# An expert loop over pairs, written out and pipelined, with a flipped token gather, a 14-slot weight ring and 8 KB rows

## The reference: an attention block with 16 experts, then a second block

```
cap = CAPACITY_FACTOR * seq // N_EXPERTS            # 2*512/16 = 64 tokens per expert
aff = softmax(h @ w_router)                          # 512 x 16
gate, idx = top_k(aff.T, cap)                        # per expert: 64 tokens and their gates
xe = h[idx]                                          # 16 x 64 x 1024
a  = silu(xe @ w_gate[e]) * (xe @ w_up[e])           # 1024 -> 1024, twice
ye = (a @ w_down[e]) * gate[..., None]
y  = zeros(512, 1024).at[idx].add(ye)                # scatter back, added to x
```

## Time and profile before

| | |
|---|---|
| median of three runs | 1732.81 us (1731.86 to 1734.91) |
| profiled execution, span from first to last instruction | 1732.2 us (no other time is recorded for this execution) |
| PE busy | 1569.3 us, 91% |
| VectorE, ScalarE, GpSimd busy | 574.1, 474.7, 100.6 us |
| DMA queue of SP | 304.14 MB, 47.0% of the 16 engines' span |
| the eight passes of the expert loop on PE | from 459.6 to 974.5 us |

### The profile page before, as it was taken

The page is one execution under the profiler, slowest core; times in us unless marked ns, Lnnn a source line. Parts: engine busy times, 40 slices in busy tenths (PEclk is TensorE's granted clock), DMA queues, the critical chain, the costliest instruction groups (busy, mean ns, idle before and its releaser), DMA issues.

```text
span 1732.2 us, 18849 instructions
## 1 busy us (share of the span) xinstructions
PE 1569.3 (91%) x7428; PEld 1006.7 (58%) x7428; DVE 574.1 (33%) x1061; ACT 474.7 (27%) x855; POOL 100.6 (6%) x118
## 2 busy tenths in 40 slices
PE   6959959988499999999999789998989899999998
PEld 3434526633234434434434479996767688888886
DVE  0145365442401211211211462112556433344334
ACT  2143236611211011011101331124763433213321
POOL 2000030000000000000000120000002211000100
PEclk9979969998799999999999899998989999999999
DMA  5279360012199999999999302214011132233221
GB/s 204 30 247 380 125 230 1 2 60 75 49 402 380 384 408 377 387 405 393 387 408 381 120 25 73 74 50 146 1 37 49 49 97 98 97 98 97 98 73 49
DMA packets 105457, 305.15 MB, mean 176 GB/s; under 512 B 7052, under 2 KB 43173, under 8 KB 103346
## 3 DMA queue, kind: packets, MB, share of 16 engines
q1 hardware_dynamic: 104712, 304.14, 47.0%
q0 software_dynamic: 512, 0.09, 0.1%
q10 hardware_dynamic: 170, 0.05, 0.0%
HBM read 300.07 MB, written 4.19 MB: 176 GB/s over the span
## 4 chain that ended last, share of the span: by engine, by line
PE 83%; DVE 6%; ACT 4%; POOL 2%; DMA 2%; issue 1%; SPq 1%; ACTq 0%; DVEq 0%; POOLq 0%
PE ps L683 19%; PE ps L725 11%; PE ps L726 11%; PE ps L727 11%; PE ps L448 4%; PE ps L671 4%; PE ps L613 3%; PE ps L713 3%; PE ps L809 2%; PE ps L566 2%; ACT sb L946 2%; PE ps L574 2%; DMA sb<-in_w_mod 2%; PE ps L489 1%; PE ps L589 1%
## 5 line engine op out<-in xcount | busy, mean ns | idle before, releaser
L683 PE MATMUL ps<-sb 128*64 128x512 f32 x1536 | 334.9, 594 | 13.3 <-ACT sb L946 13.3
L683 PEld LDWEIGHTS ps<-sb 128*64 128x64 f32 x1536 | 110.1, 137 | 221.7 <-issue 214.3
L946 ACT ACTIVATE sb<-ps 128x512 f32<-128x512 f32 (+5 forms) x217 | 104.3, 485 | 423.1 <-PE ps L683 163.9
L725 PE MATMUL ps<-r_act,r_top 128*128 128x512 f32 x352 | 138.3, 393 | 3.5 <-POOL r_act L1885 2.3
L727 PE MATMUL ps<-r_act,r_low 128*128 128x512 f32 x352 | 137.3, 390 | 0.0
L1759 DVE TENSOR_TENSOR r_low<-raw,r_top 128x2048 fp32r<-128x2048 f32 x33 | 74.4, 2293 | 79.9 <-ACT r_top L946 79.9
L1582 DVE TENSOR_TENSOR sb<-sb,ps 128x512 f32<-128x512 f32 x16 | 11.0, 688 | 253.5 <-PE ps L683 253.5
L726 PE MATMUL ps<-r_low,r_mid 128*128 128x512 f32 x240 | 93.4, 389 | 0.0
L725 PE MATMUL ps<-r_low,r_h 128*128 128x256 f32 x320 | 90.7, 283 | 0.0
L726 PE MATMUL ps<-r_low,r_h 128*128 128x256 f32 x320 | 90.6, 283 | 0.0
L727 PE MATMUL ps<-r_low,r_top 128*128 128x256 f32 x288 | 81.5, 283 | 0.0
(11 more groups left out here) (353 smaller groups left out, 2393.4 us busy)
## 6 DMA issues: line engine op xcount, KB each, us to landing
sb<-in_w_gate SPq DMA_DIRECT2D x64, 1024.0 KB, 17.9
sb<-in_w_up SPq DMA_DIRECT2D x64, 1024.0 KB, 11.2
sb<-in_w_down SPq DMA_DIRECT2D x64, 1024.0 KB, 12.6
sb<-in_w_mod SPq DMA_DIRECT2D x16, 1536.0 KB, 9.4
raw<-in_f_w_up SPq DMA_DIRECT2D x22, 1024.0 KB, 7.7
raw<-in_a_w_in SPq DMA_DIRECT2D x12, 1024.0 KB, 5.4
raw<-in_f_w_down SPq DMA_DIRECT2D x5, 2048.0 KB, 7.7
sb<-in_w_in SPq DMA_DIRECT2D x4, 1440.0 KB, 10.6
```

The lines of the kernel that those rows point to most:

```text
L683: mm = pe.matmul(PS[64 * hf:64 * hf + 64, b * HALF:(b + 1) * HALF], lhsT(k), ring[:, c % RINGN, kk, hf * HALF:(hf + 1) * HALF], start=(k = ...
L725: pe.matmul(o, a_hi, b_hi, start=first, stop=False)
L946: return act_(o, i_, ACT.Identity, bias=bias, scale=scale)
```

## The change

The loop over pairs becomes straight code with another order on PE, SP, ScalarE and VectorE.

- **Gather flipped.** `onehot` (fp32r) is now the loaded operand, and the token rows, split once into `h2hi` and `h2lo`, are the moving one, 512 columns at a time: 16 fp32r matmuls for a pair (`gather`, after-line L648). Four small ones (L653) fetch the gate of each slot into `gcol`. The result `xe` has tokens on partitions, and eight transposes (`turn_xe`, L664) turn it. ScalarE makes `h2hi` with four copies, VectorE `h2lo` with four subtractions, ahead of the loop.
- **Gate folded.** The expert output is multiplied by `gcol` and split into `yehi` (ScalarE) and `yelo` (VectorE). `GT` is a plain one-hot, and the scatter is 16 fp32r matmuls (L684, L685) over two PSUM banks instead of four. The matmul L665 is gone, L663 is now fp32r (L720).
- **Pipelined.** The gather of the next pair stands behind this pair's fourth matrix, its transposes ahead of the sixth. The scatter of the last pair is spread behind eight chunks of matrices 2 and 3.
- **Ring.** 14 slots instead of 12. Partition p now takes rows 2p and 2p+1 of a chunk, one row of 8 KB (`expert_load`, L2008); the transposes read every second column to match.
- **Ends.** Slot numbers run from 1, which drops L1548 and the copy L1534. `xc` is loaded behind the last chunk, into slot 10, and normalised by ScalarE and VectorE inside the last pair. The first three weight pieces of the second block are issued right behind it.

```diff
-RINGN = 12
+RINGN = 14
...
+            def gather(i):
+                pe.wait_ge(*at("x_onehot", i))
+                for hf in range(2):
...
+                        for part in (h2hi, h2lo):
+                            mm = pe.matmul(bank(6 + hf), onehot[:, t, :], part[t][:, hf * HALF:(hf + 1) * HALF],
+                                           start=(t == 0 and part is h2hi), stop=(t == NT - 1 and part is h2lo))
...
+            for i in range(PAIRS):
...
+                weights(i, 0, claim(0, ("x_sil", (i, 0))), tokens(0))
+                weights(i, 1, claim(1, ("x_act", (i, 0))), tokens(0), adds=0)
+                weights(i, 2, claim(2, ("x_sil", (i, 1))), tokens(1), adds=4)
+                turn_act(i, 0)
...
+                weights(i, 3, claim(0, ("x_act", (i, 1))), tokens(1))
+                if i + 1 < PAIRS:
+                    gather(i + 1)
+                pe.wait_ge(*at("x_aT", (i, 0)))
+                weights(i, 4, claim(1, ("x_ye_a", (i, 0)), ("x_ye_d", (i, 0))), hidden(0))
+                turn_act(i, 1)
+                if i + 1 < PAIRS:
+                    turn_xe(i + 1)
+                pe.wait_ge(*at("x_aT", (i, 1)))
+                weights(i, 5, claim(2, ("x_ye_a", (i, 1)), ("x_ye_d", (i, 1))), hidden(1))
+            for n in range(8):
+                scatter(PAIRS - 1, n)
```

On ScalarE, in each pair (the `else` branch is the last pair):

```diff
+                copy(actT[:, 0, :, :], bank(3).rearrange("p (k q) -> p k q", k=4)).then_inc(*inc("x_aT", (i, 0)))
+                if i + 1 < PAIRS:
+                    x_rows(i + 1)
+                else:
+                    eng.wait_ge(*at("xc_in"))
+                    for t in range(NCT):
+                        a = act_(sb(T16 + t * D, D), xc[t], ACT.Square, accum_out=ssq[:, 12 + t:13 + t])
+                    a.then_inc(*inc("ssqc"))
+                    eng.wait_ge(*at("rsce"))
+                    act_(rs[:, 12:14], rs[:, 12:14], ACT.Sqrt).then_inc(*inc("rscs"))
+                eng.wait_ge(*at("x_pe_aT", (i, 1)))
+                copy(actT[:, 1, :, :], bank(3).rearrange("p (k q) -> p k q", k=4)).then_inc(*inc("x_aT", (i, 1)))
```

On SP, the layout of a chunk and the end of the loads:

```diff
-            gate = [I[n].rearrange("a e (c j p) f -> (a e) c p j f", p=P, j=2) for n in ("w_gate", "w_up", "w_down")]
+            experts = [I[n].rearrange("a e (c p j) f -> (a e) c p (j f)", p=P, j=2) for n in ("w_gate", "w_up", "w_down")]
...
+            for c in range(12, NCHUNK):
+                expert_load(c)
+            sp.wait_ge(*at("x_used", NCHUNK - RINGN))
             for t in range(NCT):
                 sp.dma_start(xc[t], I["ctx_2"][0, t * P:(t + 1) * P, :]).then_inc(*inc("xc_in", 0, 16))
```

More of the change, by code:

```diff
@@ L116, in value @@
         return self.known.get((name, key), 1)
[L120 to L138, removed]
     def result(self):
-        return {**self.here, **{("total", n): c for n, c in self.count.items()}}
+        return dict(self.here)
 def constants():
     ident = np.eye(P, dtype=np.float32)
-    slot = np.tile(np.arange(CAP, dtype=np.float32), (P, 1))
-    slotc = (np.arange(P) % CAP).astype(np.float32)[:, None]
+    slot = np.tile(np.arange(1, CAP + 1, dtype=np.float32), (P, 1))
+    slotc = (np.arange(P) % CAP + 1).astype(np.float32)[:, None]
     pos = np.arange(S, dtype=np.float32)
@@ L243, in program @@
         max8 = small(2, 8)
-        selcur = small(P)
+        gcol = small(2)
         relb = small(AH)
@@ L286, in program @@
         rows16 = sb(QKV + 4096, 2, S)
-        affT, work = rows16[0:16, 0, :], rows16[0:16, 1, :]
+        scan16, work = rows16[0:16, 0, :], rows16[0:16, 1, :]
         pos_row = sb(QKV + 7168, 2, S)
[L289 to L300, removed]
+        sel, lgrow = pos_row[0:16, 0, :], pos_row[0:16, 1, :]
+        SLOT_AT = [RING + SLOT * n for n in range(12)] + [QKV, QKV + SLOT]
+        ring = [sb(o, 2, D) for o in SLOT_AT]
+        posr = place("r_posr", TABS, S, F32R)[0:16, :]
+        selcur = place("r_selcur", SELCUR, P, F32R)[0:16, :]
+        h2hi = [place(f"r_h2hi{t}", T16 + t * D, D, F32R) for t in range(NT)]
+        h2lo = [place(f"r_h2lo{t}", Z + t * D, D, F32R) for t in range(NT)]
+        xeT = sb(Z + 4096, KD, P)
+        act = sb(Z + 5120, S)
+        YEHI, YE = QKV + 4096, QKV + 5120
+        yehi = place("r_yehi", YEHI, D, F32R)
+        yelo = place("r_yelo", YE, D, F32R)
+        ye = sb(YE, D)
+        xe = sb(QKV + 6144, D)
+        actT = sb(QKV + 7168, 2, 4, P)
+        GT = place("r_gt", SPARE, S, F32R)
+        sil = sb(SPARE + 512, S)
+        onehot = view(place("r_onehot", SPARE + 1024, NT * P, F32R)[:, :], NT)
         vm = sb(12288, 6, D)
@@ L641, in _ @@
                 tr.then_inc(*inc("pe_" + name))
[L644 to L666, removed]
-                for j in range(2):
[L668 to L716, removed]
@@ new lines, in weights @@
+            def weights(i, n, b, lhsT, adds=None):
+                for ch in range(4):
+                    c = 24 * i + 4 * n + ch
+                    pe.wait_ge(*at(f"w_slot{c % RINGN}", c))
+                    for kk in range(2):
+                        k = 2 * ch + kk
+                        for hf in range(2):
+                            mm = pe.matmul(PS[64 * hf:64 * hf + 64, b * HALF:(b + 1) * HALF], lhsT(k),
+                                           ring[c % RINGN][:, kk, hf * HALF:(hf + 1) * HALF],
+                                           start=(k == 0), stop=(k == KD - 1), skip_group_check=True)
+                    mm.then_inc(*inc("x_used", c))
+                    if adds is not None and i:
+                        scatter(i - 1, adds + ch)
@@ L1133, in _ @@
[L1133 to L1148 removed]
+            copy(work, PS[0:16, bank_of["affT"] * HALF:(bank_of["affT"] + 1) * HALF]).then_inc(*inc("affT"))
@@ L1157, in _ @@
             for t in range(NT):
-                eng.wait_ge(*M.last("x_add", 2 * t + 1))
+                eng.wait_ge(*at("x_add", (PAIRS - 1, 2 * t + 1)))
                 if t:
@@ L1519, in _ @@
                 h2_evac(t)
+            for t in range(NT):
+                eng.wait_ge(*at("pe_h2T", (t, 1)))
+                eng.wait_ge(*at("h2hi", t))
+                ve.tensor_tensor(h2lo[t][:, :], h2[:, t, :], h2hi[t][:, :].bitcast(F32), ALU.subtract).then_inc(*inc("h2lo", t))
             eng.wait_ge(*at("pe_lgT"))
@@ L1594, in _ @@
+            for n in range(8):
+                add_rows(PAIRS - 1, n)
             eng.wait_ge(*at("wg_hi"))
```

269 lines of the change are left out of this document (173 added, 96 removed).

## The result

The changed kernel takes 1703.33 us (median of 4 runs, 1698.74 to 1704.81) against 1732.88 us before: a ratio of 0.9831, 95% interval 0.9815 to 0.9848, that is 29.5 us faster. The forecast was 1700.4 us.

A forecast was written before the change was run, and what follows sets the result against it. PE bound the loop before; after the change the weight stream would. Stream start 469.7 plus 444 us for 178 chunks plus a 28.7 us tail ends at 942.8, 32.4 us sooner: 1700.4 us, range 1684 to 1716.

The forecast's parts named there:

- PE before, the stream 3 us behind: Expert loop before: PE's own sequence is the bound, 64.5 us by pass; the weight stream needs 61.4 us.
- PE's new sum, 52.3 us a pair: Changed expert loop: PE's work per pair sums to 52.3 us, below the stream's 61.4, so DMA becomes the bound.
- The lead of PE, four to five pairs: Changed loop: PE starts with 14 chunks in hand and waits for chunks only after four to five pairs.
- The rate, 420 GB/s between bounds of 410 and 428: Weight stream with 8 KB rows: 420 GB/s, a chunk 2.50 us, 178 of them 444 us.
- Start: Head of the loop: first matrix at 465.8 instead of 473.0 us, 7.2 us sooner; h2hi and h2lo hidden.
- Tail: After the last chunk at 914 us: context tiles land late, 28.7 us follow, last addition at 942.8 instead of 975.2.
- Behind the loop: nothing: After the last additions: no further change; span 1699.8 us, plus 0.6 us between span and median.
- The rival of the clock: Loop: PE waiting for chunks may drop the granted clock; gain gone at mean 0.84, 1759 us at 0.80; chance 0.05.

The follow-up runs named there:

- e10_before_rows_only: Kernel before with rows of 8 KB alone and no stride, output not the reference's: 1730.84 us, ratio 1.0001 to before.
- experiment 4: Changed kernel, every chunk from the fifteenth on loading only the first 4 KB of each 8 KB row, output not the reference's: 1667.52 us, ratio 0.9637 to before.
- experiment 3: Changed kernel with each gather product made twice in pairs 1 to 7, output not the reference's: 1704.44 us, ratio 0.984 to before.
- experiment 2: Changed kernel with the old chunk layout, two rows of 4 KB in a partition, and transposes without stride: 1716.19 us, ratio 0.9915 to before.
- Experiment 1: Changed kernel with ScalarE's context-tile work moved behind its last yehi and VectorE's behind the last eight additions: 1692.17 us, ratio 0.9776 to before.

## Why the prediction was right, point by point

- **PE before, the stream 3 us behind.** Right. The kernel before with the longer rows alone (`e10_before_rows_only`) shows a faster stream worth nothing there, and experiment 4 shows what PE alone would need now.
- **PE's new sum, 52.3 us a pair.** 2.9 us too low: 55.2 measured. The gather was right (16 starts, 0.23 us apart, 3.7 us). The mis-sized term is the scatter when it stands between the chunks. I took 0.46 us for its two matmuls and 1.73 for a chunk. The timeline of the changed kernel shows 2.53 for both together, 0.34 more, eight times a pair, 2.7 of the 2.9 us:

```profile
526.64 1.94 PE L696 MATMUL ps<-sb 128*64 128x512 f32 x8
528.50 0.50 PE L684 MATMUL ps<-r_yehi,r_gt 128*128 128x512 f32 x1
528.84 0.40 PE L685 MATMUL ps<-r_yelo,r_gt 128*128 128x512 f32 x1
529.17 1.94 PE L696 MATMUL ps<-sb 128*64 128x512 f32 x8
```

  It cost nothing, as experiment 3 with 3.7 us more cost nothing.
- **The lead of PE, four to five pairs.** Met, but by luck. I divided the 14 chunks in hand (35 us) by a gain of 7.7 us a pair. The real gain is 59.7 - 55.2 = 4.5 us, and the same division gives over seven pairs. Yet PE first waits at 687.6 us, ahead of the fifth chunk of the fifth pair:

```profile
688.22 1.94 PE L696 MATMUL ps<-sb 128*64 128x512 f32 x8 [0.63 <-ACT sb L1162]
```

  (The profile names ScalarE; but that chunk is the 87th of the stream, which by 2.49 us each from my 469.7 on would land at 686.3, and the later waits of this pair are put down to the weight DMA.) The division left out that the stream starts 4 us behind PE, that the first pair, without a scatter, is 6 us shorter (21.4 instead of 27.6 us from its first matrix to the slot numbers of L720), and that PE uses up the chunks of a pair unevenly. With my 52.3 us a pair the same count, an estimate, has the waits begin already in the fourth pair.
- **The rate, 420 GB/s between bounds of 410 and 428.** Measured 421. Both the row of 5.76 KB (425) and that of 4 KB (410) were good neighbours; the one of 12 KB (377 and 427) was no guide. The Trainium skill ("DMA: Bandwidth & Descriptors", section "Why small descriptors are slow (HBM only)") allowed an estimated 415; the runs show 421 with 8 KB and 410 with 4 KB in the same code (experiment 2), so the rule makes the difference too small here.
- **Start.** First matrix at 465.65 (465.8), first load issued at 467.62 (467.95). Two errors cancel in it: the gather began at 456.69 instead of 457.3, and it took 6.1 us instead of 5.5, as 11 of its 16 matmuls, not 8, ran at the lower clock. `h2hi` and `h2lo` stayed hidden.
- **Tail.** Tiles landed at 918.5 (916.8), then 4.2 us to the matrix (4.6), 8.74 us for it (9.6: the lower clock cost 1.6 us, not 2.5), 3.8 to the scatter (3.3), 8.3 for it (8.4). Last addition 943.5 (942.8). Experiment 1 shows the cause: without that wait it ends 13.7 us sooner, in place of the 15.2 I gave.
- **Behind the loop: nothing.** Right: 31.7 us at the last addition, 31.2 in the span. What the forecast missed is what lies around the span: the profiled execution took 1.75 us more than its span, and the median was 2.3 us above it, where I had carried over the 0.6 us between median and span of before. That is 1.7 of the 2.9 us between 1700.4 and 1703.3.
- **The rival of the clock** did not come. In the windows with the most waits PE was busy 17.8 of 20 us, with waits of some 0.5 us ahead of a chunk, at a granted 1.00. In the loop the clock fell only where PE stood idle for 14 us, at 900 to 920 us (0.81). The 0.79 that I held up for this rival is of a window in which PE was busy for all of its 8 us; the waits lie in the windows ahead of it.

## What to carry to other kernels

When a second resource stands a few per cent behind the first, sum both before crediting an edit: here 9.3 us a pair came off PE (64.5 to 55.2) and 4.8 of them counted (64.5 to 59.7), and from then on only bytes, rate and slots moved the time of the loop. A work item that is moved into a long queue inherits the whole queue: look at which in-order engine waits for its landing, and what stands behind that wait; 4.2 us of ScalarE and VectorE work, put behind the last landing and ahead of PE's last matrix, cost 9.5 to 11 us, while the whole change gained 29.5. And try an edit alone where it should be worth nothing: that is how the price of the stride came to light, which the full change hid.

## What the runs showed of the hardware that I had not expected

- A loaded operand read with a stride of two float32 columns slows PE: at a granted 1.00 the 64 records of a gather took 7.75 instead of 7.36 us, 5% more, and the kernel before with the stride took 0.41% (0.29 to 0.54) more.
- Two fp32r matmuls on the whole array between two chunks of float32 matmuls on half of it cost 0.34 us beyond the sum of both (2.53 us for a group that sums to 2.19). Whether the type or the width of the array does it, no run separates; going from the same chunks to float32 transposes on the whole array, the trace shows 0.14 us (7.02 us for a matrix of 32 records that follow one another at 0.215).
- One row of 8 KB in place of two of 4 KB moves 421 instead of 410 GB/s, in a saturated queue as well as in short windows (424 to 427 against 412 to 415).
